# A mixture-of-experts layer on one core: the last job's down product by column half, with its weighing, addition and statistics after each half

## The reference, cut to what matters

```python
def expert_block(args):
    tok, e = args
    xb = xt[tok]
    gate = jnp.minimum(xb @ w_gate[e] + b_gate[e], SWIGLU_LIMIT)
    up = jnp.clip(xb @ w_up[e] + b_up[e], -SWIGLU_LIMIT, SWIGLU_LIMIT)
    act = (up + 1.0) * gate * jax.nn.sigmoid(SWIGLU_ALPHA * gate)
    return act @ w_down[e] + b_down[e]
...
y_rows = y_rows.reshape(n_rows, D) * row_weight[:, None]
y = jnp.zeros_like(xt).at[row_token].add(y_rows)
...
x = layer_norm(DEEPNORM_ALPHA * x + g2 * moe_ffn(...), ln2_g, ln2_b)
```

## Time and profile before

| what | value |
|---|---|
| time, median of three runs | 2314.98 us (2314.53 to 2316.0) |
| the profiled execution's own time | 2311.77 us |
| its span | 2309.8 us |
| TensorE busy, share of the span | 2170.6 us, 94% |
| VectorE busy | 1028.4 us, 45% |
| mean granted TensorE clock | 0.972 |
| last down product, start to end in the chain of waits | 2274.70 to 2290.12 us |
| last instruction of `finish(2)` ends | 2301.06 us |
| the three output writes of GpSimd start | 2292.12, 2296.74 and 2301.84 us |

### The profile page before, as it was taken

One profiled execution on the slowest core, in us unless ns is written; L12 is line 12 of the kernel. 1 busy time (PEld: TensorE's weight loads), 2 busy tenths in 40 slices (PEclk: granted clock), 3 DMA queues, 4 the chain that ended last, 5 costly groups with the idle time before them and its releaser, 6 DMA issues.

```text
span 2309.8 us, 35457 instructions
## 1 busy us (share of the span) xinstructions
PE 2170.6 (94%) x9927; PEld 1009.2 (44%) x9928; DVE 1028.4 (45%) x1591; ACT 477.8 (21%) x646; POOL 452.6 (20%) x422
## 2 busy tenths in 40 slices
PE   6999999889959999999999899999998999999995
PEld 3444444564544444443443344444443444444442
DVE  2665745556674333444334243422345333222346
ACT  2343447331210111111111111111111111101134
POOL 0011100002221222222222132311213212212212
PEclk9999999889959999999999999999999999999998
DMA  9212320012344676779479999857899747897673
GB/s 353 78 56 74 109 64 28 1 74 94 109 192 146 242 288 215 292 277 400 147 271 399 372 339 406 297 164 236 279 371 352 262 159 248 296 321 242 205 284 132
DMA packets 169785, 512.34 MB, mean 222 GB/s; under 512 B 16815, under 2 KB 51383, under 8 KB 168586
## 3 DMA queue, kind: packets, MB, share of 16 engines
q1 hardware_dynamic: 152290, 468.96, 54.4%
q0 software_dynamic: 15840, 37.45, 7.3%
q10 hardware_dynamic: 1608, 5.29, 0.6%
HBM read 482.08 MB, written 32.51 MB: 223 GB/s over the span
## 4 chain that ended last, share of the span: by engine, by line
PE 87%; DVE 5%; DMA 3%; SPq 2%; issue 2%; ACT 1%; POOLq 0%; DVEq 0%; POOL 0%; ACTq 0%
PE psall L580 27%; PE psall L608 14%; PE psall L584 10%; PE psall L765 10%; PE psall L612 5%; PE psall L589 4%; PE psall L753 3%; PE psall L872 2%; PE psall L866 2%; DMA arena<-in_w_down_dram 2%; PE psall L617 2%; PE psall L649 1%; PE psall L732 1%; SPq L430 1%; DVE arena L1491 1%
## 5 line engine op out<-in xcount | busy, mean ns | idle before, releaser
L580 PE MATMUL psall<-arena 128*128 128x512 f32 x1472 | 645.6, 597 | 23.7 <-issue 19.0
L580 PEld LDWEIGHTS psall<-arena 128*128 128x128 f32 x1472 | 278.7, 191 | 369.1 <-issue 362.8
L608 PE MATMUL psall<-arena 128*128 128x512 f32 x736 | 322.3, 596 | 5.2 <-issue 2.6
L584 PE MATMUL psall<-arena 128*64 128x512 f32 x1152 | 256.1, 595 | 6.2 <-DMA arena<-in_w_up_dram 2.1
L1663 DVE STREAM_TRANSPOSE arena<-arena 128x1024 f32<-128x1024 f32 x49 | 61.0, 1245 | 446.6 <-PE psall L580 276.5
L765 PE MATMUL psall<-arena 128*128 128x512 f32 (+1 forms) x560 | 230.5, 569 | 0.0
L608 PEld LDWEIGHTS psall<-arena 128*128 128x128 f32 x736 | 139.2, 191 | 182.8 <-issue 181.0
L1249 ACT COPY arena<-psall 128x512 f32<-128x512 f32 x49 | 28.7, 586 | 725.3 <-PE psall L649 725.3
L1862 DVE COPY arena<-psall 128x512 f32<-128x512 f32 x48 | 33.2, 691 | 314.7 <-PE psall L649 308.4
L1261 ACT ACTIVATE arena<-arena 128x1024 f32<-128x1024 f32 x49 | 51.8, 1057 | 571.0 <-DVE arena L1690 571.0
L1973 POOL DMA_INDIRECT arena<-h_rows,lruw x144 | 147.1, 1022 | 82.7 <-POOL lruw L1966 39.4
(11 more groups left out here) (332 smaller groups left out, 2132.2 us busy)
## 6 DMA issues: line engine op xcount, KB each, us to landing
arena<-in_w_gate_dram SPq DMA_DIRECT2D x128, 1024.0 KB, 6.8
arena<-in_w_up_dram SPq DMA_DIRECT2D x128, 1024.0 KB, 7.9
arena<-in_w_down_dram SPq DMA_DIRECT2D x128, 1024.0 KB, 9.5
arena<-in_w_ada_dram SPq DMA_DIRECT2D x16, 1024.0 KB, 5.3
arena<-in_w_ada_dram SPq DMA_DIRECT2D x4, 2048.0 KB, 15.1
arena<-in_x_dram SPq DMA_DIRECT2D x16, 512.0 KB, 6.8
arena<-in_w_in_dram SPq DMA_DIRECT2D x16, 512.0 KB, 3.9
arena<-in_w_out_dram SPq DMA_DIRECT2D x1, 4096.0 KB, 13.9
```

The costliest lines, as they stand in the source:

```text
L580: mm = pe.matmul(ps[2 * g + s], xT[:, k, :], w[:, s * BANK:(s + 1) * BANK], start=(k == 0), stop=(k == KD - 1))
L584: mm = pe.matmul(ps[2 * g][HT * j:HT * j + HT, :], xT[:, k, 0:HT], w[:, j * BANK:(j + 1) * BANK], start=(k == 0), stop=(k == KD - 1), skip ...
L608: mm = pe.matmul(ps[6 + s], aT[:, k, :], w[:, s * BANK:(s + 1) * BANK], start=(k == 0), stop=(k == KD - 1))
```

## The change

On TensorE a new function `down_last` does the down product of the trip in which no job is current. It runs all eight row blocks for columns 0 to 511 first, then all eight for columns 512 to 1023, and gives two steps of `dn_used` after each half instead of one after each pair of row blocks. It is reached by a test of `typ_c` in every trip, ahead of the `by_kind` of `down`. On VectorE `weigh_last` goes by the same halves: for each, wait for its half of the product, add the bias, weigh, add to set 2 of the late rows (the first half waits for `late_in` there), and take the statistics of the half. The joining of the statistics, and the step of `var_ready` that lets ScalarE take the root, move into `weigh_last` too, and with it ahead of `finish(1)`.

```diff
--- before.py
+++ after.py
@@ -620,6 +620,19 @@
                     if k % 2 and sweep == sweeps[-1]:
                         mm.then_inc(dn_used, 1)
 
+        def down_last(pe, u, order_):
+            pe.wait_ge(aT_act, u + 1)
+            pe.wait_ge(aT_dve, u + 1)
+            pe.wait_ge(y_biased, u + 1)
+            for s in range(2):
+                for k in range(KD):
+                    if k % 2 == 0 and s == 0:
+                        pe.wait_ge(d_dn[k // 2], order_)
+                        settle(pe)
+                    mm = pe.matmul(ps[6 + s], aT[:, k, :], ring[GUP + k // 2][:, k % 2, s * BANK:(s + 1) * BANK],
+                                   start=(k == 0), stop=(k == KD - 1))
+                mm.then_inc(dn_used, DNP // 2)
+
         def by_kind(eng, t, what):
             with eng.If(t > 2):
                 with eng.If(t > 3):
@@ -982,7 +995,11 @@
                                 pe.nop()
                             by_kind(pe, t, lambda kind: gate_up(pe, kind, u, on_, GUP // 2, GUP))
                             job_row(pe, [typ_n, ord_n], u + 2)
-                            by_kind(pe, tp, lambda kind: down(pe, kind, u, op_))
+                            with pe.If(typ_of(pe, typ_c) > 0):
+                                by_kind(pe, tp, lambda kind: down(pe, kind, u, op_))
+                            with pe.Else():
+                                down_last(pe, u, op_)
+                            pe.nop()
                             for to, of in ((typ_p, typ_c), (ord_p, ord_c), (typ_c, typ_n), (ord_c, ord_n)):
                                 pe.reg_mov(to, of)
                         pe.nop()
@@ -1654,10 +1671,20 @@
 
             def weigh_last(u, order_):
                 link(dve.tensor_copy(wcol, row_w[:, 0, ds(u, 1)]))
-                dve.wait_ge(dn_used, u * DNP + DNP)
                 dve.wait_ge(bdn_spread, order_)
-                link(dve.tensor_tensor(gb, psY, ebias[:, 2], ALU.add))
-                link(dve.scalar_tensor_tensor(out=gb, in0=gb, scalar=wcol, in1=adarow[:, 3], op0=ALU.mult, op1=ALU.mult))
+                for h in range(2):
+                    b = slice(h * BANK, (h + 1) * BANK)
+                    dve.wait_ge(dn_used, u * DNP + (h + 1) * (DNP // 2))
+                    settle(dve)
+                    link(dve.tensor_tensor(gb[:, b], psY[:, b], ebias[:, 2, b], ALU.add))
+                    link(dve.scalar_tensor_tensor(out=gb[:, b], in0=gb[:, b], scalar=wcol, in1=adarow[:, 3, b], op0=ALU.mult,
+                                                  op1=ALU.mult))
+                    if h == 0:
+                        dve.wait_ge(late_in, 48)
+                    link(dve.tensor_tensor(late[:, 2, b], late[:, 2, b], gb[:, b], ALU.add))
+                    link(dve.bn_stats(st[:, 6 * h:6 * h + 6], late[:, 2, b]))
+                link(dve.bn_aggr(mv, st))
+                dve.nop().then_inc(var_ready, 1)
 
             def turn_rows_in():
                 dve.transpose(xT.rearrange("p b (t s) -> p t b s", t=4), xg.rearrange("p (t b i) -> p t b i", t=4, b=KD)).then_inc(xT_ready, 1)
@@ -1874,12 +1901,6 @@
                                     weigh_last(u, ord_of(dve, ord_p, wait_p))
                                     dve.wait_ge(row_sq, NT + 2)
                                     finish(1, late_neg[:, 1:2], ALU.add)
-                                    dve.wait_ge(late_in, 48)
-                                    link(dve.tensor_tensor(late[:, 2], late[:, 2], gb, ALU.add))
-                                    for q in range(2):
-                                        link(dve.bn_stats(st[:, 6 * q:6 * q + 6], late[:, 2, q * BANK:(q + 1) * BANK]))
-                                    link(dve.bn_aggr(mv, st))
-                                    dve.nop().then_inc(var_ready, 1)
                                     finish(2, mv[:, 0:1], ALU.subtract)
                                 dve.nop()
                             with dve.If(typ_of(dve, typ_n) > 0):
```

## The result

The changed kernel takes 2321.26 us (median of 11 runs, 2319.17 to 2322.16); the kernel before, timed beside it, 2315.25 us (11 runs, 2313.52 to 2318.64). The ratio is 1.0023, 95% interval [1.0014, 1.0032]: 6.0 us slower by the medians. The profiled execution took 2319.95 us with a span of 2318.0 us, against 2311.77 and 2309.8 before.

A forecast was written before the change was run, and what follows sets the result against it. TensorE's matmuls were taken to hold 87% of the chain, with VectorE and then the chained output writes bounding the end. Tail -0.9 and test +0.5 gave -0.4 us: 2314.98 to 2314.6 us, range 2311.7 to 2317.9.

The forecast's parts named there:

- The tail: After the last down product: the third output write starts at 2300.96 instead of 2301.84, a gain of 0.9 us.
- The test in every trip: TensorE's job loop: the added compare shows only at 9 down products already idle on issue; +0.5 us, at most 1.2.
- The last product: Last down product on TensorE: again runs its first records slower, 15.41 us, so its end stays at 2290.12.
- The distance from the profile to the median: Whole kernel: the timed median stands 3.2 us above the profiled execution, and this distance is kept.
- A: Output writes at the end: they don't bind, VectorE's 1.7 us come through whole; 2313.8 us, chance 0.17.
- B: Last trip: down_last's code is loaded when first reached and TensorE stalls, some 1.5 us; 2316.1 us, chance 0.12.
- C: TensorE's job loop: no longer held whole, one code load each trip costs 71 us; 2386 us, chance 0.05.
- D: VectorE's last halves: they do not overlap as the first waits for later gathers; 2317.6 us at 3 us, chance 0.04.

The follow-up runs named there:

- test in mid trip: The changed kernel with its test moved ahead of the second half of the gate and up products, down_last still last in the code; 2319.42 us, ratio 1.0018.
- Compare alone: The kernel before with one always-true test ahead of the down product in every trip, no second copy of the product; 2318.48 us, ratio 1.0011.
- three compares: The kernel before with three nested always-true tests ahead of the down product in every trip, no second copy; 2327.62 us, ratio 1.0045.
- last branch first: The changed kernel, test ahead of the second gate and up half and inverted, so down_last stands ahead of the normal path; 2336.37 us, ratio 1.0097.

## Why the prediction was wrong

*The tail, -0.9 us: right.* It measured -1.05, by the mechanism forecast: the second write's landing holds up the third, which starts 10.68 us after the product's end (forecast 10.8, before 11.7), and `finish(2)` ends 8.7 us after it (forecast 9.2). Two pairs that differ in VectorE's order show 1.1 us each (18.65 against 19.75; 18.68 against 19.78, where TensorE's order differs too). That it came so near has some luck in it: the second half began 0.15 us after the product's end instead of 0.5, since the slow product here ended 2.5 us after the gathers, and the second write took 2.85 us to land instead of 2.6. The version with the test in mid trip shows how close that was.

*The test in every trip, +0.5 us with an upper bound of 1.2: the step that failed.* It held that "one more compare can only show" at the 9 down products with idle time that is already there, 5.9 us, and priced the compare as a share of that idle time, 0.06 to 0.13 us a place. Both are wrong. At those 9 places the step measures 0.2 us each, 1.8 in all, which is over the bound by itself. Six more entries behind short matmuls show it too, 1.6 us: two of them had 0.14 to 0.15 us of idle time before, which the list leaves out, and four had none in at least one of the two profiles. In all it is 15 entries at 0.22 us, 3.3 us. No idle time does not mean that there is slack. In the kernel before, the sequencer reaches the table read only 1.0 to 1.5 us before the array runs out of work behind a quarter sweep, but 7.4 us before behind a full gate and up product; from there to the first matmul it needs 1.4 us or more. So behind a quarter sweep each step more shows in full, and behind a full product none does.

The forecast also said that the trace shows no such instruction by itself. It does: the compares of `by_kind` stand in it as steps of the sequencer, and from their records the price of one compare could have been read. A compare that doesn't jump takes 65 to 77 ns, and the next step starts 0.12 to 0.14 us after its start; the register move ahead of it takes another 0.09 us. The Trainium skill gives 108 ns for a compare-and-branch ("Advanced Engine Details and Errata", Control Flow Timing), which lies between the two figures for the compare alone; the 0.21 to 0.22 us of an entry are the compare and the move together.

*A cost that had no term: the way out of the trip.* The code of kinds 1 and 2 now ends with a jump past the second copy, one step more, which the orders shown ahead of the prediction don't reach, so it was priced at nothing. It runs in 18 trips. The aligned timelines show it at 8 trip ends, six behind a quarter down product and two behind a half one, with 0.23 to 0.47 us, 2.5 us in all; the four above 0.3 are those where a round of the outer loop begins. Compare alone and three compares have neither the jump nor the steps at those places; each version with the copy behind the normal path has both. So it is not code that is passed over which costs there, but an instruction that runs.

The two sum to 5.8 us. Some 2 us of that are given back where TensorE waits for loads (around 1246 to 1264, and 1767 us), and small differences elsewhere make up the rest; the loop stretch is 4.2 us longer than in the second profile of before (1431.64 against 1427.47).

*The last product, "runs its first records slower and will again": true, but not by the same amount.* It took 16.65 us instead of 15.40. The granted clock in one microsecond (columns as above), 3 us into the product before the change:

```profile
2277.70:2278.70 1.00, 1.00 (x3) 0.38 (x2) 0.96 (x3) 0.99 (x2) 1.00 (x1) 1.00 0.00 0
```

And 4 us into it after the change:

```profile
2286.70:2287.70 1.00, 1.00 (x2) 0.34 (x1) 1.00 (x2) 0.22 (x1) 0.82 (x1) 0.50 0.00 0
```

Before, TensorE is already at 2.4 GHz (1.00); after, still at 1.2. In these two profiles that ate the tail's gain. The order by halves isn't what sets it: the old order took 15.40 to 16.50 us, halves 13.97 to 17.00. Eleven of the thirteen profiles fall into two groups, 15.4 to 15.7 and 16.3 to 17.0 us, and either group has both orders, with a test and without one. What sets it stays open, and with it whether these 1.3 us belong to the change.

The account, means of the two profiles of each kernel: loop stretch +5.5, last product +1.3, tail -1.1, the rest of the way +0.8, which is 6.5 us of span against 6.0 timed. By the second profile of before alone, which shares the stall with both of after, it is +3.9, +1.3, -1.1 and +1.1, or 5.2 us. The rest lies for the most part ahead of the loop stretch, before 797 us, and no experiment looked into it.

*The distance from the profile to the median* was kept at 3.2 us. That profile was an execution without the stall; the second, with it, took 2314.44.

*The rivals.* A: no, the landing binds, in every version with VectorE by halves. B: no; ScalarE's idle time at the start of the last trip is 2.41 us as against 2.43, and the last product waits for ScalarE's copy as before (1.69 us, before 1.61). C: its sign was right and its mechanism exists (last branch first), but not in this kernel; what made it slower was no load. D: not here, but in the two versions with the test in mid trip (tails of 22.29 and 22.84 us).

## What to carry to other kernels

A step more in an engine's instruction stream is priced by the places where its sequencer is just in time, not by the idle time that the profile lists; the stretches behind many short matmuls are such places, and each compare with its register move cost 0.22 us there. Read the sequencer's own steps at such a place, and count the jumps at the end of a branch as well as the test at its head. A case for the last trip alone belongs behind the loop, where the other trips neither test for it nor jump over it. Profile the kernel before twice: a stall that comes and goes was worth 3 us, more than any term of this sum.

## What the runs showed of the hardware

- Behind 64 matmuls of 57 ns (3.66 us), a register move and a compare-and-branch ahead of the next matmul cost 0.21 to 0.22 us of TensorE's time, and three such pairs 0.67. The compare's own record is 65 to 77 ns long.
- The jump past the second copy took 169 ns, and the next step of TensorE's sequencer started 0.23 us after its start.
- In the kernel before, TensorE's sequencer reached the table read 1.0 to 1.5 us ahead of the array's end of work behind a quarter sweep, and 7.4 us ahead behind a full gate and up product. The read took 0.53 to 0.61 us at most places, and 1.7 to 2.0 us at four.
- TensorE's loop ran 1350 us without an instruction packet after it had grown by the copy; with the same copy ahead of the normal path, 9 packets came twice, at some 8.3 and 7.5 us, of which 2.4 us each were a product at the lower clock behind the idle time.
- The last product began below full clock in all profiles but two (those with the test in mid trip, 13.97 us). In the other eleven it took 15.40 to 17.00 us, in either order.
